# Two more slabs of the input projection by seven products, their steps taken out of the attention, and a head norm whose inverse root is exp(-ln/2) on ScalarE

## What is computed

```
h   = rmsnorm(x)
(q, k_c, v_c, k_s, v_s, k_w, v_w, g_nsa, mq, mk, mv, mo, mi, mf, cu) = split(h @ w_in)
a   = head_rmsnorm(nsa_attention(q, ...), 16 heads)      # compressed, selected and windowed keys, three gates
hm  = head_rmsnorm(sigmoid(mo) * mlstm(silu(conv(mq, mk)), mv, mi, mf), 4 heads)
c   = silu(layernorm(depthwise_conv31(ca * sigmoid(cg))))
x   = x + concat(a, hm, c) @ w_out
x   = x + hierarchical_moe(rmsnorm(x))                    # 32 experts of hidden size 512, top 2 of one group
out = rmsnorm(x)
```

## Time and profile before

| | |
|---|---|
| median of 3 runs | 1415.66 us (1415.53 to 1416.2) |
| the profiled execution's own time | 1415.79 us |
| its span, first to last instruction | 1414.0 us |
| TensorE matmuls busy | 1197.9 us (85%) |
| VectorE busy | 492.0 us (35%) |
| ScalarE busy | 253.3 us (18%) |
| mean granted TensorE clock | 0.938 |
| read from HBM | 476.05 MB |

### The profile page before, as it was taken

The page is one execution under the profiler, slowest core; times in us unless marked ns, Lnnn a source line. Parts: engine busy times, 40 slices in busy tenths (PEclk is TensorE's granted clock), DMA queues, the critical chain, the costliest instruction groups (busy, mean ns, idle before and its releaser), DMA issues.

```text
span 1414.0 us, 18072 instructions
## 1 busy us (share of the span) xinstructions
PE 1197.9 (85%) x7497; PEld 707.3 (50%) x7497; DVE 492.0 (35%) x1020; ACT 253.3 (18%) x628; POOL 20.1 (1%) x88
## 2 busy tenths in 40 slices
PE   8999999999999998669599958769587695876977
PEld 7999999776568753233244314224142241422422
DVE  5599997663866421111010210111101111011113
ACT  3001111534500221011111102002020020200212
POOL 2000000000010000000000000000000000000001
PEclk9999999999999999879999988989899798897988
DMA  9958577430654899999999999999999999999996
GB/s 302 322 180 166 152 161 239 119 93 27 180 119 183 358 423 425 429 427 427 429 427 429 426 427 428 428 429 426 428 427 428 428 427 428 427 428 428 427 427 278
DMA packets 133827, 479.35 MB, mean 339 GB/s; under 512 B 48012, under 2 KB 105840, under 8 KB 108272
## 3 DMA queue, kind: packets, MB, share of 16 engines
q1 hardware_dynamic: 127104, 477.58, 86.7%
q10 hardware_dynamic: 6640, 0.58, 0.4%
HBM read 476.05 MB, written 2.10 MB: 338 GB/s over the span
## 4 chain that ended last, share of the span: by engine, by line
PE 54%; DMA 43%; DVE 1%; ACT 1%; issue 1%; ACTq 0%; DVEq 0%
DMA ring<-in_expert_w_up_dram 36%; PE PS L1149 14%; PE PS L1490 10%; DMA spare<-in_expert_w_up_dram 7%; PE PS L1298 5%; PE PS L1191 3%; PE PS L1477 3%; PE PS L1275 2%; PE PS L1683 2%; PE PS L1468 1%; PE PS L1693 1%; PE PS L1141 1%; PE PS L972 1%; PE PS L1210 1%; PE PS L1554 1%; PE PS L1250 1%
## 5 line engine op out<-in xcount | busy, mean ns | idle before, releaser
L1490 PE MATMUL PS<-ring,XG 128*32 128x512 f32 x1296 | 224.4, 736 | 143.8 <-DMA ring<-in_expert_w_up_dram 104.5
L1490 PEld LDWEIGHTS PS<-ring,XG 128*32 128x32 f32 x1296 | 57.3, 131 | 271.1 <-issue 268.0
L3166 DVE TENSOR_TENSOR hTe<-PS,sg 128x128 f32<-128x128 f32 (+1 forms) x31 | 9.9, 319 | 347.1 <-ACT sg L2272 346.9
L2982 DVE TENSOR_TENSOR x<-PS,x 128x1024 f32<-128x1024 f32 x41 | 50.2, 1224 | 210.0 <-PE PS L1571 208.7
L2259 ACT ACTIVATE Hs<-PS 128x512 f32<-128x512 f32 x30 | 17.9, 597 | 463.0 <-PE PS L1490 349.2
L1477 PE MATMUL PS<-ring,XG 128*64 128x512 f32 x192 | 84.6, 594 | 18.3 <-DMA ring<-in_expert_w_up_dram 15.1
L1571 PE MATMUL PS<-Y,SW 128*128 128x512 f32 (+2 forms) x176 | 90.7, 627 | 1.5 <-ACT ro L2368 1.5
L1490 PE MATMUL PS<-spare,XG 128*32 128x512 f32 x208 | 68.7, 820 | 26.7 <-DMA ring<-in_expert_w_up_dram 26.6
L1479 PE MATMUL PS<-ring,XG 128*64 128x512 f32 x192 | 85.0, 595 | 0.0
L1468 PEld LDWEIGHTS PS<-sel,xn 128*128 128x128 f32 x640 | 75.3, 191 | 12.9 <-issue 12.7
L1149 PE MATMUL PS<-hT,ring 128*128 128x128 f32 x672 | 78.8, 275 | 0.0
(11 more groups left out here) (512 smaller groups left out, 1564.9 us busy)
## 6 DMA issues: line engine op xcount, KB each, us to landing
ring<-in_expert_w_up_dram SPq DMA_DIRECT2D x53, 2048.0 KB, 23.7
ring<-in_expert_w_gate_dram SPq DMA_DIRECT2D x53, 2048.0 KB, 27.1
ring<-in_expert_w_down_dram SPq DMA_DIRECT2D x51, 2048.0 KB, 26.6
ring<-in_w_in_dram SPq DMA_DIRECT2D x17, 2048.0 KB, 10.6
spare<-in_expert_w_gate_dram SPq DMA_DIRECT2D x9, 2048.0 KB, 25.5
spare<-in_expert_w_up_dram SPq DMA_DIRECT2D x8, 2048.0 KB, 23.5
spare<-in_expert_w_down_dram SPq DMA_DIRECT2D x8, 2048.0 KB, 27.6
ring<-in_w_in_dram SPq DMA_DIRECT2D x16, 512.0 KB, 7.3
```

The source lines that it names most:

```text
L1490: mm = pe.matmul(PS[r:r + 32, 0, :], gathered_rows(q, 4 * c + j)[:, column:column + 32], weight_rows(slots[u], 4 * (c % 2) + j), start=(c ...
L2982: dve.tensor_tensor(y, new, old, ALU.add).then_inc(sc_added, 1)
```

## The change

The slabs `mv0` and `mv1` join `FAST_SLABS` and `LATE` moves to the first `mo` unit, so 64 late steps are left. Their weight sums need other room than `mv` and `mo`: for slab 16 and 17 of the fast ones `in_t2` is `att[:, 0:1024]`, `in_t3` is `att[:, 3072:4096]` and `mo`. `follow(15)`, `follow(16)` and `finish(17)` replace `finish(15)`. The order on TensorE is written anew with fewer fills; the convolution's share of the output part is cut in quarters between the scores of step 3, and the features 0 to 3 of one token tile are multiplied between `attend(2)` and `attend(3)`. ScalarE's saves of late units are fewer. `head_root` takes a logarithm and an exponential with scale -0.5, the second waiting for the first, in place of a square root, and `head_norm` has no reciprocal.

```
-FAST_SLABS = (..., "q3", "vw0")
+FAST_SLABS = (..., "q3", "vw0", "mv0", "mv1")
-LATE = units_before("mv")
+LATE = units_before("mo")
...
-        in_t3, in_t2 = (... for tile in (mv, mo))
+        mv_k, mo_k = (... for tile in (mv, mo))
+        att_low, att_high = (att[:, c:c + 1024].rearrange("p (k n) -> p k n", k=8) for c in (0, 3072))
+        MV = len(FAST) - 2
+
+        def in_t3(j):
+            return {MV: att_high, MV + 1: mo_k}.get(j, mv_k)
+
+        def in_t2(j):
+            return att_low if j >= MV else mo_k
...
-            def scores(s, steps):
+            def scores(s, steps, between=None):
...
                         fill(steps)
+                        if between is not None:
+                            between(i)
...
+            def conv_quarter(i):
+
+                out_part(i // 2, conv_f[2 * (i % 2):2 * (i % 2) + 2], i % 2 == 0, False)
+
-            fill(8)
+            fill(4)
             pe.wait_ge(unit_saved, LATE)
             pe.wait_ge(cmp_saved, 3)
             scores(0, 2)
-            scores(1, 3)
-            fill(16)
+            scores(1, 2)
+            fill(12)
             pe.wait_ge(sT_ready, ML_H)
-            attend(0, 4)
-            scores(2, 3)
-            attend(1, 4)
+            attend(0, 0)
+            scores(2, 4)
+            attend(1, 0)
             mean_square(0)
-            scores(3, 3)
-            fill(LATE_STEPS)
-            mlstm_values()
             pe.wait_ge(conv_out, CT)
             pe.wait_ge(unit_saved, len(UNITS))
-            out_part(0, conv_f, True, False)
+            scores(3, 0, conv_quarter)
+            mlstm_values()
             mean_square(1)
             attend(2, 0)
-            out_part(1, conv_f, True, False)
+            out_part(0, head_f[0:4], False, False)
             attend(3, 0)
             mlstm_columns()
             mean_square(2)
             pe.wait_ge(hm_out, ML_H)
-            out_part(0, ml_f + head_f, False, True)
+            out_part(0, ml_f + head_f[4:8], False, True)
             mean_square(3)
             out_part(1, ml_f + head_f, False, True)
...
             def head_root(s):
                 act.wait_ge(oms_done, s + 1)
-                act.activation(PS[:, 6 + s % 2, :], PS[:, 6 + s % 2, :], ACT.Sqrt, bias=EPS_C).then_inc(oroot, 1)
+                r = PS[:, 6 + s % 2, :]
+                step(act.activation(r, r, ACT.Ln, bias=EPS_C))
+                act.activation(r, r, ACT.Exp, bias=ZERO_C, scale=-0.5).then_inc(oroot, 1)
 
             exponents(0, 0)
             late_saves(1)
-            exponents(1, 1)
+            exponents(1, 0)
             late_saves(2)
-            attend_saves(0, 1)
+            attend_saves(0, 0)
             exponents(2, 0)
             late_saves(1)
-            attend_saves(1, 1)
+            attend_saves(1, 0)
             head_root(0)
             exponents(3, 0)
-            late_saves(1)
             act.wait_ge(unit_saved, len(UNITS))
             act.activation(mo[:, :, :], mo[:, :, :], ACT.Sigmoid, bias=ZERO_C).then_inc(mo_gated, 1)
             head_root(1)
...
-            finish(15)
+            follow(15)
+            follow(16)
+            finish(17)
...
                 dve.wait_ge(oroot, s + 1)
-                step(dve.reciprocal(r, r))
```

More of the change, by code:

```diff
@@ L191 @@
 UNITS = projection_units()
-FAST_SLABS = ("cg1", "ca0", "ca1", "mq0", "mq1", "mk0", "mk1", "vc0", "ks0", "kw0", "vs0", "q0", "q1", "q2", "q3", "vw0")
+FAST_SLABS = ("cg1", "ca0", "ca1", "mq0", "mq1", "mk0", "mk1", "vc0", "ks0", "kw0", "vs0", "q0", "q1", "q2", "q3", "vw0", "mv0",
+              "mv1")
 FAST = [u for u, (n, _, kind, _, i) in enumerate(UNITS) if SLABS[n] in FAST_SLABS and i == 0]
@@ L433, in build @@
         tok_21, tok_22 = hT[:, 0:8, P:2 * P], hT[:, 8:16, P:2 * P]
-        in_t3, in_t2 = (tile[:, :, :].rearrange("p a b -> p (a b)").rearrange("p (k n) -> p k n", k=8) for tile in (mv, mo))
+        mv_k, mo_k = (tile[:, :, :].rearrange("p a b -> p (a b)").rearrange("p (k n) -> p k n", k=8) for tile in (mv, mo))
+        att_low, att_high = (att[:, c:c + 1024].rearrange("p (k n) -> p k n", k=8) for c in (0, 3072))
[4 more added lines that the diff above has]
+            return att_low if j >= MV else mo_k
         def quarter(u, high, right):
@@ L1164, in fast_products @@
                 fast_product(u, "m5", tok_s1, quarter(u, 0, 1)).then_inc(prod_done, 1)
-                fast_product(u, "m7", tok_s3, in_t3)
+                fast_product(u, "m7", tok_s3, in_t3(j))
                 pe.wait_ge(w_summed, 4 * j + 3)
-                fast_product(u, "m6", tok_s2, in_t2)
+                fast_product(u, "m6", tok_s2, in_t2(j))
                 pe.wait_ge(w_summed, 4 * j + 4)
@@ L2466, in left_sums @@
                     dve.wait_ge(unit_done, FAST[j - 1] + 2)
-                dve.tensor_tensor(in_t3, quarter(u, 1, 1), quarter(u, 0, 1), ALU.subtract)\
+                dve.tensor_tensor(in_t3(j), quarter(u, 1, 1), quarter(u, 0, 1), ALU.subtract)\
                     .then_inc(w_summed, 1)
@@ L2474, in right_sum @@
                 dve.wait_ge(w_summed, 4 * j + 2)
-                dve.tensor_tensor(in_t2, quarter(u, 1, 1), quarter(u, 0, 1), ALU.subtract)\
+                dve.tensor_tensor(in_t2(j), quarter(u, 1, 1), quarter(u, 0, 1), ALU.subtract)\
                     .then_inc(w_summed, 1)
@@ L2481, in last_sum @@
                 dve.wait_ge(w_summed, 4 * j + 3)
-                dve.tensor_tensor(quarter(u, 1, 0), quarter(u, 1, 0), in_t2, ALU.subtract)\
+                dve.tensor_tensor(quarter(u, 1, 0), quarter(u, 1, 0), in_t2(j), ALU.subtract)\
                     .then_inc(w_summed, 1)
```

## The result

The changed kernel takes 1424.61 us (median of 4 runs, 1424.27 to 1424.9) against 1415.88 (4 runs, 1415.53 to 1416.2): ratio 1.0062, 95% interval 1.005 to 1.0074, 8.7 us slower. The profiled execution took 1424.27 us against 1415.79. The prediction was 1422.1 and slower; the time lies inside its range, 2.5 us from its value.

What follows compares the result with a forecast made beforehand. TensorE bounds the kernel until the later output columns at 404.70, then expert-weight transfers of fixed length. Those columns move to 410.8, plus 0.2 for the router's root: +6.3 on 1415.79 gives 1422.1 us, range 1417.5 to 1426.

Steps and rivals of the forecast that it cites:

- step 1: Two fast mv slabs after mlstm_turn take 25.0 us; TensorE then waits 0.5 and scores start at 288.6.
- steps 1, 3, 5 and 7: TensorE's waits: 0.5 us before the first scores, 2.3 before attend(0), 1.3 in attend(1), 3.7 in attend(2).
- Steps 1 to 6: From the two slabs to mean_square(1): scores start 288.6, last maximum 318.0, attend(0) 325.6, mlstm_values 367.5, end 371.2.
- The rival of the bias ring: Long score steps: maxima could come closer than 3.63 us, saving up to 7.2, total 1414.9; chance 0.15.
- Step 7: ScalarE ahead of attend(2): sigmoid, then two loads per root; second block at 376.3, wait 3.7 us, attend(2) ends 380.5.
- the case of one load: Rival at the head roots: logarithm and exponential share one table load, copies 1.1 us earlier, total 1421.0; chance 0.22.
- The clock's rival: New TensorE waits lower the granted clock to 0.8 for 40 us from 371 on: 8 us more, 1430; chance 0.05.
- VectorE's tail: Last head norms: cover 0.7 us; rival says later roots make output features 4 to 7 wait, up to 1424.5; chance 0.10.
- Step 8 and 9: Output part of four features and attend(3) until mlstm_columns at 390.3, then 20.5 us to later columns at 410.8.
- Step 10: The router norm's root needs a table load in an idle time of 0.88 us; costs 0.2 us.

Runs made afterwards that it cites:

- Experiment 6: Changed kernel with its 64 late steps respread: fill(17) ahead of attend(0), one step per pair in scores(2), seven after it; 1421.48 us, ratio 1.0039.
- experiment 4: Changed kernel with the output part of features 0 to 3 placed ahead of attend(2) instead of behind it; 1419.59 us, ratio 1.0028.
- e5: Changed kernel with the mLSTM gate's sigmoid taken on ScalarE right after the saves of attend(1), ahead of the first root; 1421.53 us, ratio 1.0043.
- Experiment 1: Changed kernel with four matmuls on unused data while TensorE waits in attend(2); 1422.71 us, ratio 1.0052.
- e2: Changed kernel with square root and reciprocal put back in place of logarithm and exponential; 1426.79 us, ratio 1.0079.
- e10: Changed kernel, reordered (output parts, sigmoid and mLSTM root earlier, late steps respread), with square root and reciprocal put back; 1427.61 us, ratio 1.0089.
- e3: Kernel before with logarithm and exponential and no reciprocal as its only change; 1419.57 us, ratio 1.003.

## Why the prediction was right, and by how much it missed

**The saving and where it went.** The two slabs take 25.03 us, as in step 1. The 3.2 us of matmul saved did not reach the end, because the 64 steps had also been the cover of waits: steps 1, 3, 5 and 7 forecast 0.5, 2.3, 1.3 and 3.7, and the trace has 0.54, 2.19, 1.66 and 4.32. Experiment 6 shows the second and third to be for want of fillers: the steps left, laid elsewhere, give 3.1 us back (2.1 by its profile). Experiments 4 and 5 show the fourth to be ScalarE's queue ahead of the copies: an independent output part under it gives 5.0, a shorter queue 3.1.

**Steps 1 to 6.** Scores started at 288.21 (288.6 forecast, and the slabs started 0.43 earlier), the last maximum at 317.66 (318.0), `attend(0)` at 325.25 (325.6), the second block of `attend(1)` at 347.79 (348.0), `mlstm_values` at 367.33 (367.5); `mean_square(1)` ended at 370.9 (371.2). The maxima of VectorE in after, columns as in the earlier trace rows:

```profile
291.50 1.22 DVE L2736 TENSOR_REDUCE rs<-spare 128x4 f32<-128x1024 f32 x1
295.13 1.22 DVE L2736 TENSOR_REDUCE rs<-spare 128x4 f32<-128x1024 f32 x1
298.76 1.22 DVE L2736 TENSOR_REDUCE rs<-spare 128x4 f32<-128x1024 f32 x1
```

They come 3.63 apart with two steps between pairs. The rival of the bias ring, a shorter period, is refuted.

**Step 7: two loads per root, and the wait.** One load of 1.28 stands before the logarithm and another before the exponential, in all four roots, so the case of one load is refuted. The rows of before only had the order exponential, logarithm; that the forecast took two for the other order was a choice that came true, not something read. The Trainium skill (ScalarE: Activation LUTs, Table sets) has the two functions in one set; ScalarE's timeline of after does not bear that out for this kernel, in this order either. The second block was forecast at 376.3 and came at 376.23; the wait is 4.32 and not 3.7 because TensorE was there 0.7 earlier (371.9 against 372.6), which costs nothing.

**The step that was mis-sized** is the end of step 7, "`attend(2)` ends 4.2 later (367.38 to 371.60) at 380.5". It took 6.8 us, since the granted clock was 0.58 over it: 2.6 us missed. The duration was read from a stretch in which TensorE had not waited, and was used behind a wait of 4.3. The clock's rival named the mechanism, but gave it the wrong size: 0.8 for 40 us and 8 us, where it is the lower level for 6.8 us and 2.6 us. The argument against it, a largest wait "under 4 us", was no argument: the wait was 4.32, and experiment 4 shows a fall behind 2.19. Experiment 1 measures the term by itself. The range of the forecast did not allow for it: it was wide enough for the missing 2.6 us because of other cases (VectorE's tail above all), and that is luck.

**Step 8 and 9.** From the output part of four features to the columns 9.7 us (383.10 to 392.80) were measured and 9.8 forecast (380.5 to 390.3); from there to the later columns 20.6, and 20.5 forecast. Of the sum, 410.8 + 2.6 = 413.4: that is the measured 413.41; the slabs' start, 0.43 earlier, was used up by the time ScalarE's exponentials ended (forecast 369.2, measured 369.25).

**VectorE's tail** did not bind: its last head norm ended at 409.18 (408.07 + 1.11), and by the forecast's own spacing TensorE reached those features at 410.0. The cover of 0.8 us is the 0.7 of the forecast. Experiments 2 and 10 show what is behind it: with the reciprocals back it binds by 2.68 and 3.30. The saving on VectorE was thus needed in this order, and its price on ScalarE could be hidden.

**Step 10.** From the later columns to the first matmul of line 1477 (line 1464 in before), a place behind the router's root, it is 88.68 us in after and 88.59 in before. The root's new load was forecast at 0.2; the difference is 0.1.

## What to carry to other kernels

Work that is poured into waits is worth its time only once: making it cheaper and smaller uncovers the waits, so count the cover that is left at each hand-over, and lay independent work that is to be done anyway (here an output part) under the longest of them. A function exchanged on ScalarE costs its table loads where a copy for TensorE is queued behind it; move what stands ahead of that copy first. A wait of TensorE of a few microseconds can be paid twice, once idle and once in the matmuls behind it, so read durations for such a place from rows at the lower clock, and look for it in windows of a few microseconds, not in the page's slices.

## What the runs showed of the hardware that was not expected

A single idle time of TensorE of 4.32 us, behind 24 us without a wait at a granted clock of 1.00, is followed by 6.8 us at 0.58 (eight transposes 1.97 instead of 1.14), and then by 1.00 again. Keeping TensorE at work on unused data in the wait removes it. A fall is also seen behind shorter waits: 2.92 and 2.68 us in e2 (0.75 and 0.69 in the windows behind them), 2.91 and 3.30 in e10 (0.79 in 370 to 378 us, 0.54 in 409.6 to 416.4). Behind waits of about 2.2 us the fall comes in some executions and not in others: it is there before `attend(0)` in e4 (0.66) and e5 (0.69 in 325 to 330 us) and absent in after, e1 and e2, with the same instructions and the same wait. Behind the two profiled waits of 2.37 (e3 and e5) it is absent. What decides between these stays open.
